# RMS norms of a 256-token network on one core: residuals and squares in two halves of 512 columns

## The chip, the cores and the metric

The kernel runs on one core of a Trainium2 chip. The core has a matrix engine (TensorE, PE in the profile; its weight loads are PEld), a vector engine (VectorE, DVE), a scalar engine (ScalarE, ACT), GpSimd (POOL) and SyncE (SP), which here only issues transfers. The engines run their own instruction streams side by side and meet at semaphores. The metric is the device time of one execution in microseconds (us); of several runs the median counts.

## The reference, cut to what matters

A batch of one sequence with S = 256 tokens and D = 1024 features passes through two blocks in float32. Every sublayer is fed by an RMS norm:

```
def rms_norm(x, g):
    y = xf * lax.rsqrt(jnp.mean(xf * xf, axis=-1, keepdims=True) + EPS)
    return y * g
first_block:   h = h + even_mixer(norm(h));  h = h + swiglu(norm(h))
               h = h + odd_mixer(norm(h));   h = h + moe_swiglu(norm(h));  h = norm_final(h)
second_block, twice:
    x = x + 0.5 * norm(swiglu_2(norm(x)));  x = x + norm(hybrid_mix(norm(x)))
    x = x + 0.5 * norm(swiglu_2(norm(x)))
```

So there are eleven norms of the residual stream itself: one of the input, three behind the plain residual additions of the first block, the final norm of the first block behind its mixture of experts, and six in the second block, each ahead of a sublayer. The first of those six stands directly behind the final norm of block one. In the second block each sublayer's output also has a norm of its own (post) before it is added; that one is not touched here.

## The kernel before, in words

The residual stream H is 128 partitions x 2 token tiles x 1024 columns; a token tile t is 128 tokens. All weights stream from memory through a ring of six buffers (SP issues, ACT rounds to a high part at L1360, DVE makes the low part at L1914), and PE multiplies high and low parts (L584, L581 for projections, L600 and L612 for the gated feed-forward, L757 and L783 for the experts).

The order of work on each engine is written out by hand; nothing is planned at run time, and every engine executes its stream in order. At each border between sublayers it is as follows.

- **DVE makes the residual.** `residual` (L2148) adds the two PSUM banks of a tile into H[:, t, :], in one instruction of 1024 columns, for t = 0 and then t = 1. In the second block `post` does it: ahead of the border it forms y * gain in HN (L2167), then for each tile a root's inverse (`inverse_root`, L1951 to L1953, and one product at L2175) and one fused multiply-add over 1024 columns (L2177). After the experts, four multiply-adds of 512 columns (L2075, `add_expert`) add the last expert. Each finished tile counts up `h_ready`.
- **ACT makes the sum of squares.** `norm` waits for `h_ready` and calls `mean_square`: a Square over 1024 columns whose accumulator gives the sum (L1379, ACTIVATE and ACTIVATION_READ_ACCUMULATOR in the trace), then a Sqrt of that sum with EPS as its bias (L1382).
- **DVE makes the diagonal.** `norm` on DVE adds EPS to the sum (L1959), takes the reciprocal of ACT's root with one Newton step (L1951 to L1953) and writes DIAG[:, t, :], the identity times the inverse root (L1962). This is behind both residual tiles in DVE's stream.
- **PE transposes and scales** at once: `turn_norm` (L815) multiplies the columns of H[:, t, :] with DIAG[:, t, :], 16 of the trace's matmuls for tile 0 and then 16 for tile 1; it has nothing else to do from the end of the old sublayer until DIAG of tile 0 is there.
- ACT (L1390) and DVE (L1971) evict the four banks into XHI and XLO with the gains, and PE starts the next sublayer.

Two borders differ. At the start, x is loaded tile by tile (`x_loaded`) and there is no residual. Behind the experts, the final norm scales H itself (L2805 to L2809: the inverse root and a multiply of 1024 columns per tile, which counts up `h_ready` again), and the next norm follows at once. The last `post` has no norm behind it: SP waits for all of `h_ready` and writes the output (L434).

Of the kernel before, what the change touches and what calls it, by code (L numbers as in the profile page):

```python
# [8 lines left out]
ALU = mybir.AluOpType  # L9
ACT = mybir.ActivationFunctionType  # L10
# [4 lines left out]
TT = S // P  # L15
D = 1024
KT = D // P
F_DENSE = 2816 // P
NE = 8
# [4 lines left out]
EPS = 1e-6  # L24
# [29 lines left out]
def build(nc, A, out):  # L54

    ctx = ExitStack()
    with ctx:
# [63 lines left out]
        H = sb("h", [P, TT, D])  # L121
# [17 lines left out]
        GBC = sb("gbc", [P, 2, D])  # L139
# [27 lines left out]
        EPS_COL, SCRATCH_COL = STAT[:, 60:61], STAT[:, 61:62]  # L167

        names = """hi_ready lo_ready chunk_used bank_free silu_ready hidhi_made
        hid_ready h_ready y_ready ssq_ready root_of_ssq y_ssq y_gained y_mean root_of_y diag_ready tp_ready xhi_ready x_ready ident_ready first_tp first_ready consts_ready cols_tp cols_ready  # L170
        loads_done gbc_used dve_order act_order pool_order router_ready msk_ready pos_mm flag_ready
        hng_ready hnh_ready hnl_ready psel_ready first_gath xgh_ready xgl_ready m_silu m_hid m_tp m_hidhi m_hidlo
        aux_mm aux_free yeh_ready yel_ready last_comb d_silu d_hid d_tp d_hidhi d_hidlo
# [198 lines left out]
        @block.sync  # L372
        def _(sp):
            def load(c_, slot, src):
                if not isinstance(c_, int) or c_ >= RING:
                    sp.wait_ge(s["lo_ready"], c_ - RING + 1)
                sp.dma_start(RAW[:, slot, :].rearrange("p (k n) -> p k n", k=src.shape[1]) if src.shape[1] * src.shape[2] == 1024
                             else RAW[:, slot, 0:src.shape[1] * src.shape[2]].rearrange("p (k n) -> p k n", k=src.shape[1]),
                             src).then_inc(raw_full[slot], 16)

            def columns(w, at_, n):
                return w[:, bass.ds(at_, n)].rearrange("(k p) n -> p k n", p=P)

            def rows(w, at_):
                return w[bass.ds(at_, P), :].rearrange("p (k n) -> p k n", k=1)

            sp.dma_start(FIRST_ROWS, vec(A["norm_mix"][0])).then_inc(first_loaded, 16)
            for t in range(TT):
                sp.dma_start(H[:, t, :], A["x"][0, t * P:(t + 1) * P, :]).then_inc(x_loaded[t], 16)
            for ph in plan:  # L390
                c0 = ph["c0"]
                if ph["kind"] == "proj":
                    for _, n, pieces in ph["units"]:
                        for i, x, k0, kn in pieces:
                            load(c0 + i, (c0 + i) % RING, columns(ph["w"][k0 * P:(k0 + kn) * P, :], x, n))
                elif ph["kind"] == "out":
                    for i, kt in enumerate(ph.get("order", range(KT))):
                        load(c0 + i, (c0 + i) % RING, rows(ph["w"], kt * P))
                elif ph["kind"] == "moe":
                    for G in range(N_GROUPS + 1):  # L400
                        e, g = divmod(G, GROUPS)
                        if G < N_GROUPS:
                            for a, w in enumerate((ph["w1"], ph["w3"])):
                                for j in range(4):
                                    c_ = m_chunk(G, 4 * a + j)
                                    src = w[e][2 * j * P:(2 * j + 2) * P, g * GW:(g + 1) * GW]
                                    load(c_, c_ % RING, src.rearrange("(k p) n -> p k n", p=P))
                        if G > 0:
                            e, g = divmod(G - 1, GROUPS)
                            for j in range(4):  # L410
                                c_ = m_chunk(G, (8 if G < N_GROUPS else 0) + j)
                                load(c_, c_ % RING, rows(ph["w2"][e], g * GW + j * P))
                else:
                    F = ph["tiles"]
                    w1, w3 = ph["w1"].rearrange("e k n -> e k n"), ph["w3"]
                    w2 = ph["w2"].rearrange("e f n -> (e f) n")

                    def w13(e, j, c_, slot):
                        for w in (w1, w3):
                            load(c_, slot % RING, columns(w[e], j * P, P))  # L420
                            c_, slot = c_ + 1, slot + 1

                    w13(0, 0, c0, c0)
                    w13(0, 1, c0 + 2, c0 + 2)
                    load(c0 + 4, (c0 + 4) % RING, rows(w2, 0))
                    with sp.Fori(1, F // 2) as i:
                        b = c0 + 6 * i - 1
                        w13(0, 2 * i, b, c0 + 5)
                        load(b + 2, (c0 + 7) % RING, rows(w2, (2 * i - 1) * P))
                        w13(0, 2 * i + 1, b + 3, c0 + 8)  # L430
                        load(b + 5, (c0 + 10) % RING, rows(w2, (2 * i) * P))
                    load(c0 + 3 * F - 1, (c0 + 3 * F - 1) % RING, rows(w2, (F - 1) * P))
            sp.wait_ge(s["h_ready"], 2 * 11)
            sp.dma_start(out[0].rearrange("(t p) d -> p t d", p=P), H[:, :, :]).then_inc(s["out_done"], 16)  # L434
            sp.wait_ge(s["out_done"], 16)

# [912 lines left out]
        def _(act):  # L1349
# [21 lines left out]

            def norm():
                for t in range(TT):
                    act.wait_ge(s["h_ready"], nxt("h_ready"))
                    mean_square(t)

            def mean_square(t):

                af(HN[:, t, :], H[:, t, :], ACT.Square, scale=D ** -0.5, accum_out=STAT[:, t:t + 1])\  # L1379
                    .then_inc(s["ssq_ready"], 1)  # L1380
                act.wait_ge(s["ssq_ready"], nxt("ssq_ready"))
                af(STAT[:, 34 + t:35 + t], STAT[:, t:t + 1], ACT.Sqrt, bias=EPS_COL).then_inc(s["root_of_ssq"], 1)  # L1382

            def gain(name):

# [473 lines left out]
            load_root()  # L1859
            for t in range(TT):  # L1860
                act.wait_ge(x_loaded[t], 16)
                mean_square(t)
            ahead(-1)
            act.wait_ge(s["first_ready"], 1)
            gain("norm_mix0")
# [34 lines left out]
        def _(dve):  # L1900
# [47 lines left out]
            def inverse_root(root, at, half, whole):  # L1948
# [4 lines left out]
                link(V_.tensor_scalar(c_, h, -half, whole, ALU.mult, ALU.add))  # L1953
                return y, c_

            def norm(keep=False):
                for t in range(TT):
                    dve.wait_ge(s["ssq_ready"], nxt("ssq_ready"))
                    link(V_.tensor_scalar(STAT[:, 36 + t:37 + t], STAT[:, t:t + 1], EPS, None, ALU.add))  # L1959
                    dve.wait_ge(s["root_of_ssq"], nxt("root_of_ssq"))  # L1960
                    y, c_ = inverse_root(STAT[:, 34 + t:35 + t], 36 + t, 0.5, 1.5)
                    V_.tensor_scalar(DIAG[:, t, :], IDENT[:, :], y, c_, ALU.mult, ALU.mult).then_inc(s["diag_ready"], 1)  # L1962
                    if keep:
                        link(V_.tensor_tensor(STAT[:, 2 + t:3 + t], y, c_, ALU.mult))
# [85 lines left out]
            def moe_sparse():  # L2050
# [81 lines left out]
                for t in range(TT):  # L2132
                    for h in range(2):
                        dve.wait_ge(s["last_comb"], 2 * t + h + 1)
                        last = add_expert(BANK[2 * t + h], NE - 1, t, h)
                    last.then_inc(s["h_ready"], 1)

            def y_wait(ph, t):

# [5 lines left out]
            def residual(ph):  # L2145
                for t in range(TT):
                    y_wait(ph, t)
                    V_.tensor_tensor(H[:, t, :], H[:, t, :], YT[t], ALU.add).then_inc(s["h_ready"], 1)  # L2148

            ngbc = [0]  # L2150

# [3 lines left out]
                ngbc[0] += 1  # L2155
                return i % 2

            def post(ph, resid):

                gi = gains_wait()  # L2160
                for t in range(TT):
# [10 lines left out]
                for t in range(TT):  # L2172
# [1 line left out]
                    y, c_ = inverse_root(STAT[:, 18 + t:19 + t], 8 + t, 0.5 * resid, 1.5 * resid)  # L2174
                    link(V_.tensor_tensor(STAT[:, 16 + t:17 + t], y, c_, ALU.mult))  # L2175
                    dve.wait_ge(s["y_gained"], nxt("y_gained", 2))
                    V_.scalar_tensor_tensor(H[:, t, :], HN[:, t, :], STAT[:, 16 + t:17 + t], H[:, t, :], ALU.mult,  # L2177
                                            ALU.add).then_inc(s["h_ready"], 1)

            def log1p(dst, e, t1, t2, t3):  # L2180

# [599 lines left out]
            V_.tensor_copy(FIRST_COLS, BANK[0][:, 0:KT]).then_inc(s["first_ready"], 1)  # L2781
            for t in range(TT):
                dve.wait_ge(x_loaded[t], 16)
            norm()
            dve.wait_ge(s["first_ready"], 1)
            ahead(-LEAD)
# [14 lines left out]

            gi = gains_wait()
            for t in range(TT):
                dve.wait_ge(s["ssq_ready"], nxt("ssq_ready"))
                link(V_.tensor_scalar(STAT[:, 36 + t:37 + t], STAT[:, t:t + 1], EPS, None, ALU.add))  # L2805
                dve.wait_ge(s["root_of_ssq"], nxt("root_of_ssq"))
                y, c_ = inverse_root(STAT[:, 34 + t:35 + t], 36 + t, 0.5, 1.5)
                link(V_.tensor_tensor(STAT[:, 2 + t:3 + t], y, c_, ALU.mult))
                V_.scalar_tensor_tensor(H[:, t, :], H[:, t, :], STAT[:, 2 + t:3 + t], GBC[:, gi, :], ALU.mult,  # L2809
                                        ALU.mult).then_inc(s["h_ready"], 1)  # L2810
            mark("gbc_used")
            mark("mixer_done")
            for l in range(2):
# [9 lines left out]
                norm()  # L2823
                gain(f"ffn2_pre{l}")
                ffn(f2)
                post(f2, 0.5)


# [32 lines left out]
```

## Time and profile before

| | us |
|---|---|
| median of 3 runs | 2709.63 (2705.88 to 2712.53) |
| the profiled execution | 2709.04 |
| its span, first to last instruction | 2707.3 |
| TensorE busy in it | 2571.3 (95%) |
| VectorE busy | 1919.0 (71%) |
| ScalarE busy | 1465.5 (54%) |
| mean granted clock of TensorE | 0.964 of full |

The difference of 1.7 us between the execution and its span lies ahead of the first and behind the last instruction. Busy shares say who could be the limit on the average; at a border between sublayers the order of the instructions and their waits decide, so those stretches have to be read by themselves.

### The profile page before, as it was taken

How to read it: one execution, taken by the hardware profiler on the slowest of the kernel's cores; microseconds unless marked ns; L12 is line 12 of the kernel's file. 1: busy time of each engine (PE TensorE's matmuls, PEld its weight loads, DVE VectorE, ACT ScalarE, POOL GpSimd, SP SyncE). 2: the span in 40 equal slices, each digit the busy share in tenths (PEclk: the TensorE clock that was granted, in tenths of full speed). 3: DMA queues.
4: the chain of work that ended last, by engine and by line, in shares of the span. 5: the costliest groups of instructions: out<-in, count | busy, mean ns of one | idle time of the engine just before them, and what ended most of it. 6: DMA issues, size and time to landing. Idle time of an engine off the chain costs nothing.

```text
span 2707.3 us, 40704 instructions
## 1 busy us (share of the span) xinstructions
PE 2571.3 (95%) x15296; PEld 2261.5 (84%) x15296; DVE 1919.0 (71%) x2609; ACT 1465.5 (54%) x1870; POOL 63.1 (2%) x137
## 2 busy tenths in 40 slices
PE   8999999699999999999999899889899899898998
PEld 8689987588888888888888799888899899787997
DVE  5555565489899989998998755687655655787554
ACT  4553353377777777777777633522533533523433
POOL 7000000000000000000000000000000000000000
PEclk9899999799999999999999899988999999989999
DMA  6255543199999999999999865422555456313553
GB/s 194 85 157 186 179 133 120 62 347 364 348 354 366 355 353 351 369 351 354 360 363 365 257 187 186 140 71 79 171 185 184 154 186 186 109 55 102 173 184 101
DMA packets 481893, 597.23 MB, mean 221 GB/s; under 512 B 21882, under 2 KB 313154, under 8 KB 481760
## 3 DMA queue, kind: packets, MB, share of 16 engines
q1 hardware_dynamic: 478048, 589.47, 64.5%
q0 software_dynamic: 3712, 6.00, 0.8%
q8 instruction: 81, 1.33, 0.2%
q14 instruction: 52, 0.43, 0.0%
HBM read 594.35 MB, written 1.05 MB: 220 GB/s over the span
## 4 chain that ended last, share of the span: by engine, by line
PE 88%; DVE 8%; ACT 2%; issue 1%; DMA 0%; DVEq 0%; SPq 0%; ACTq 0%
PE bank L600 23%; PE bank L757 23%; PE bank L783 11%; PE bank L612 11%; PE bank L584 5%; PE bank L581 2%; PE bank L815 2%; PE bank L1312 1%; DVE arena L2596 1%; PE bank L873 1%; PE bank L768 1%; DVE wlo_ring L1914 1%; PE bank L1047 1%; PE bank L704 1%; PE bank L1128 1%
## 5 line engine op out<-in xcount | busy, mean ns | idle before, releaser
L1914 DVE TENSOR_TENSOR wlo_ring<-raw_ring,whi_ring 128x1024 fp32r<-128x1024 f32 (+1 forms) x1122 | 1319.7, 1221 | 136.7 <-ACT whi_ring L1360 128.5
L1360 ACT CAST whi_ring<-raw_ring 128x1024 fp32r<-128x1024 f32 (+1 forms) x1122 | 1140.6, 1053 | 206.1 <-DMA raw_ring<-in_od_exp_w_dram 152.4
L600 PE MATMUL bank<-xhi,whi_ring 128*128 128x256 f32 x1760 | 499.6, 284 | 0.4 <-DVE xlo L1971 0.4
L600 PE MATMUL bank<-xhi,wlo_ring 128*128 128x256 f32 x1760 | 499.1, 284 | 0.0
L600 PE MATMUL bank<-xlo,whi_ring 128*128 128x256 f32 x1760 | 499.0, 284 | 0.0
L600 PEld LDWEIGHTS bank<-xhi,whi_ring 128*128 128x128 f32 x1760 | 338.0, 192 | 4.7 <-issue 0.7
L600 PEld LDWEIGHTS bank<-xlo,whi_ring 128*128 128x128 f32 x1760 | 338.0, 192 | 3.9
L600 PEld LDWEIGHTS bank<-xhi,wlo_ring 128*128 128x128 f32 x1760 | 338.0, 192 | 0.0
L1989 DVE TENSOR_TENSOR hid<-sil,bank 128x256 f32<-128x256 f32 x110 | 46.4, 422 | 402.1 <-ACT sil L1411 402.1
L1411 ACT ACTIVATE sil<-bank 128x256 f32<-128x256 f32 x110 | 42.3, 385 | 500.0 <-PE bank L600 500.0
L757 PE MATMUL bank<-whi_ring,xg0hi 128*128 128x512 f32 x448 | 180.5, 403 | 1.1 <-issue 1.1
L757 PE MATMUL bank<-whi_ring,xg1hi 128*128 128x512 f32 x448 | 180.1, 402 | 0.0
L757 PE MATMUL bank<-whi_ring,xg1lo 128*128 128x512 f32 x448 | 177.5, 396 | 0.0
L757 PE MATMUL bank<-whi_ring,xg0lo 128*128 128x512 f32 x448 | 177.5, 396 | 0.0
L757 PE MATMUL bank<-wlo_ring,xg1hi 128*128 128x512 f32 x448 | 177.4, 396 | 0.0
L757 PE MATMUL bank<-wlo_ring,xg0hi 128*128 128x512 f32 x448 | 177.3, 396 | 0.0
L584 PE MATMUL bank<-xhi,whi_ring 128*128 128x256 f32 x496 | 153.5, 309 | 0.3 <-DVE xlo L1971 0.2
L584 PE MATMUL bank<-xlo,whi_ring 128*128 128x256 f32 x496 | 146.3, 295 | 0.0
L584 PE MATMUL bank<-xhi,wlo_ring 128*128 128x256 f32 x496 | 146.3, 295 | 0.0
L783 PE MATMUL bank<-whi_ring,hidhi 128*128 128x512 f32 x448 | 139.3, 393 | 1.4 <-DVE hidlo L2097 1.4
L783 PE MATMUL bank<-whi_ring,hidlo 128*128 128x512 f32 x448 | 138.6, 391 | 0.0
L783 PE MATMUL bank<-wlo_ring,hidhi 128*128 128x512 f32 x448 | 138.2, 390 | 0.0
(502 smaller groups left out, 3858.3 us busy)
## 6 DMA issues: line engine op xcount, KB each, us to landing
raw_ring<-in_od_exp_w_dram SPq DMA_DIRECT2D x672, 512.0 KB, 5.4
raw_ring<-in_ffn_w_gate_dram SPq DMA_DIRECT2D x88, 512.0 KB, 3.9
raw_ring<-in_ffn_w_up_dram SPq DMA_DIRECT2D x88, 512.0 KB, 5.4
raw_ring<-in_ffn_w_down_dram SPq DMA_DIRECT2D x88, 512.0 KB, 5.3
raw_ring<-in_ev_ffn_w_dram SPq DMA_DIRECT2D x66, 512.0 KB, 5.2
raw_ring<-in_w_in_dram SPq DMA_DIRECT2D x42, 512.0 KB, 4.0
raw_ring<-in_od_w_in_dram SPq DMA_DIRECT2D x24, 512.0 KB, 3.9
raw_ring<-in_ev_w_in_dram SPq DMA_DIRECT2D x20, 512.0 KB, 5.2
```

Of the source, the lines that this page charges most:

```text
L581: last = mm(banks[t] if banks else row_bank(q, n, t), x[:, kt, t * P:(t + 1) * P], w[:, kk, :], start=st and (n > 256 or t == 0), stop=sp_ ...
L584: last = mm(BANK[q % 2][:, 0:S], w[:, kk, :], x[:, kt, :], start=st, stop=sp_)
L600: last = mm(BANK[qb][:, half * S:half * S + n], w[:, kt, :], x, start=(kt == 0 and a == 0), stop=(kt == KT - 1 and a == 2))
L612: last = mm(pair[h][:, :], x[:, b, t * P:(t + 1) * P], w[:, h * 512:(h + 1) * 512], start=(start and a == 0), stop=(stop and a == 2), skip ...
L704: last = mm(bank[:, q * S:(q + 1) * S], src[:, t, kt * P:(kt + 1) * P], PSEL[:, t, 2 * p:2 * p + 2, :].rearrange("p a b -> p (a b)"), star ...
L757: last = mm(bank[:, :], x[:, kt, slots], w[:, kk, :], start=(kt == 0 and a == 0), stop=(kt == KT - 1 and a == 2))
L783: last = mm(BANK[4 + h][:, :], x[:, j * P:(j + 1) * P], w[:, h * 512:(h + 1) * 512], start=(g == 0 and j == 0 and a == 0), stop=(g == GROU ...
L815: last = mm(BANK[4 + b][:, (2 * j + t) * P:(2 * j + t + 1) * P], H[:, t, kt * P:(kt + 1) * P], DIAG[:, t, :], start=True, stop=True)
L1360: nc.scalar.copy(WHI[:, slot, 0:n], RAW[:, slot, 0:n]).then_inc(s["hi_ready"], 1)
L1411: af(SIL[:, b, 0:n], BANK[b][:, 0:n], ACT.Silu).then_inc(s["silu_ready"], 1)
L1914: V_.tensor_tensor(WLO[:, slot, 0:n], RAW[:, slot, 0:n], WHI[:, slot, 0:n].bitcast(F32), ALU.subtract)\
L1989: V_.tensor_tensor(HID[:, b, 0:n], SIL[:, qb, 0:n], BANK[qb][:, S:S + n], ALU.mult)\
```

## The change

DVE writes each residual tile as two instructions of 512 columns, and each half counts up `h_ready`. ACT squares each half by itself, with a sum of its own (STAT columns t and 20 + t). DVE adds EPS to the first half's sum (`first_half`, column 22 + t, semaphore `ssq_eps`), as soon as that sum is there; ACT's Sqrt then takes the second half's sum as its input and this column as its bias. DVE's own sum for the Newton step adds the second half to it (`second_half`), where the addition of EPS stood. The places of `first_half` in DVE's stream: behind each tile's residual in `residual`, `post` (not in the last one) and behind the experts; behind each tile's arrival at the start; and in the final norm behind both scaled tiles.

```
 # ACT
-            def mean_square(t):
-                af(HN[:, t, :], H[:, t, :], ACT.Square, scale=D ** -0.5, accum_out=STAT[:, t:t + 1])\
-                    .then_inc(s["ssq_ready"], 1)
-                act.wait_ge(s["ssq_ready"], nxt("ssq_ready"))
-                af(STAT[:, 34 + t:35 + t], STAT[:, t:t + 1], ACT.Sqrt, bias=EPS_COL).then_inc(s["root_of_ssq"], 1)
+            def mean_square(t, wait_h):
+                for h in range(2):
+                    if wait_h:
+                        act.wait_ge(s["h_ready"], nxt("h_ready"))
+                    hs = slice(h * 512, (h + 1) * 512)
+                    af(HN[:, t, hs], H[:, t, hs], ACT.Square, scale=D ** -0.5,
+                       accum_out=STAT[:, 20 * h + t:20 * h + t + 1]).then_inc(s["ssq_ready"], 1)
+                act.wait_ge(s["ssq_ready"], nxt("ssq_ready", 2))
+                act.wait_ge(s["ssq_eps"], nxt("ssq_eps"))
+                af(STAT[:, 34 + t:35 + t], STAT[:, 20 + t:21 + t], ACT.Sqrt, bias=STAT[:, 22 + t:23 + t])\
+                    .then_inc(s["root_of_ssq"], 1)
 # DVE
+            def first_half(t):
+                dve.wait_ge(s["ssq_ready"], nxt("ssq_ready", 0) + 2 * t + 1)
+                V_.tensor_scalar(STAT[:, 22 + t:23 + t], STAT[:, t:t + 1], EPS, None, ALU.add).then_inc(s["ssq_eps"], 1)
+            def second_half(t):
+                dve.wait_ge(s["ssq_ready"], nxt("ssq_ready", 2))
+                dve.wait_ge(s["ssq_eps"], nxt("ssq_ready", 0) // 2)
+                link(V_.tensor_tensor(STAT[:, 36 + t:37 + t], STAT[:, 20 + t:21 + t], STAT[:, 22 + t:23 + t], ALU.add))
             def norm(keep=False):
                 for t in range(TT):
-                    dve.wait_ge(s["ssq_ready"], nxt("ssq_ready"))
-                    link(V_.tensor_scalar(STAT[:, 36 + t:37 + t], STAT[:, t:t + 1], EPS, None, ALU.add))
+                    second_half(t)
 # residual; post alike with its multiply-add, and "if not end: first_half(t)"
-                    V_.tensor_tensor(H[:, t, :], H[:, t, :], YT[t], ALU.add).then_inc(s["h_ready"], 1)
+                    for h in range(2):
+                        hs = slice(h * 512, (h + 1) * 512)
+                        V_.tensor_tensor(H[:, t, hs], H[:, t, hs], YB[t][h][:, :], ALU.add).then_inc(s["h_ready"], 1)
+                    first_half(t)
 # behind the experts
-                        last = add_expert(BANK[2 * t + h], NE - 1, t, h)
-                    last.then_inc(s["h_ready"], 1)
+                        add_expert(BANK[2 * t + h], NE - 1, t, h).then_inc(s["h_ready"], 1)
+                    first_half(t)
 # start
             for t in range(TT):
                 dve.wait_ge(x_loaded[t], 16)
+                first_half(t)
 # final norm of block one, behind the loop that scales both tiles by halves
+            for t in range(TT):
+                first_half(t)
```

## Rows read from the trace of the kernel before

**Rows 1.** Page, part 4: the chain that ended last, shares by engine.
```profile
PE 88%; DVE 8%; ACT 2%; issue 1%; DMA 0%; DVEq 0%; SPq 0%; ACTq 0%
```

**Rows 2.** Groups of instructions by form: busy us, mean ns | idle before, releaser.
```profile
L815 PE MATMUL bank<-hid,h 128*128 128x128 f32 x320 | 56.0, 357 | 57.7 <-DVE hid L1962 57.7
```

**Rows 3.** Timeline of DVE, 1728 to 1738 us: start, duration [idle before].
```profile
1730.84 1.29 DVE L2177 SCALAR_TENSOR_TENSOR h<-arena,stat,h 128x1024 f32<-128x1024 f32 x1
...
1732.92 1.28 DVE L2177 SCALAR_TENSOR_TENSOR h<-arena,stat,h 128x1024 f32<-128x1024 f32 x1
1734.12 0.15 DVE L1959 TENSOR_SCALAR stat<-stat 128x1 f32<-128x1 f32 x1
...
1735.00 0.35 DVE L1962 TENSOR_SCALAR hid<-ident,stat 128x128 f32<-128x128 f32 x1
```

**Rows 4.** Timeline of ACT, the same stretch.
```profile
1728.11 0.59 ACT L1541 ACTIVATE xlo<-bank 128x512 fp32r<-128x512 f32 x1
1728.59 0.20 ACT L1541 ACTIVATION_READ_ACCUMULATOR xlo<-bank 128x1 f32 x1
...
1732.16 1.06 ACT L1379 ACTIVATE arena<-h 128x1024 f32<-128x1024 f32 x1 [1.90 <-DVE h L2177]
1733.12 0.19 ACT L1379 ACTIVATION_READ_ACCUMULATOR arena<-h 128x1 f32 x1
1733.34 0.29 ACT L1382 ACTIVATE stat<-stat 128x1 f32<-128x1 f32 x1
```

**Rows 5.** Timelines of DVE and ACT, 150 to 164 us.
```profile
154.10 2.58 DVE L2148 TENSOR_TENSOR h<-h,bank 128x1024 f32<-128x1024 f32 x2 [4.43 <-PE bank L873]
...
156.93 0.16 DVE L1951 RECIPROCAL stat<-stat 128x1 f32<-128x1 f32 x1 [0.19 <-ACT stat L1382]
...
156.53 0.29 ACT L1382 ACTIVATE stat<-stat 128x1 f32<-128x1 f32 x1
```

**Rows 6.** Timeline of PE: the transposes at three borders.
```profile
352.06 3.84 PE L815 MATMUL bank<-hid,h 128*128 128x128 f32 x32 [2.61 <-DVE hid L1962]
...
487.17 5.47 PE L815 MATMUL bank<-hid,h 128*128 128x128 f32 x32 [2.61 <-DVE hid L1962]
...
1735.40 2.93 PE L815 MATMUL bank<-hid,h 128*128 128x128 f32 x12 [7.36 <-DVE hid L1962]
```

**Rows 7.** Groups of DVE by form.
```profile
L2075 DVE SCALAR_TENSOR_TENSOR h<-bank,arena,h 128x512 f32<-128x512 f32 x32 | 23.7, 747 | 1.8 <-PE bank L714 1.7
L2167 DVE TENSOR_TENSOR arena<-bank,gbc 128x512 f32<-128x512 f32 x24 | 15.7, 687 | 9.3 <-PE bank L612 6.8 <-PE bank L1312 2.5
L2177 DVE SCALAR_TENSOR_TENSOR h<-arena,stat,h 128x1024 f32<-128x1024 f32 x12 | 15.4, 1286 | 0.4
L2148 DVE TENSOR_TENSOR h<-h,bank 128x1024 f32<-128x1024 f32 x6 | 7.3, 1221 | 10.6 <-PE bank L1047 4.4 <-PE bank L873 4.4 <-PE bank L612 1.3
```

**Rows 8.** Timelines of ACT and DVE, 0 to 26 us.
```profile
5.04 1.06 ACT L1379 ACTIVATE arena<-h 128x1024 f32<-128x1024 f32 x1 [2.72 <-DMA h<-in_x_dram]
...
6.61 0.16 DVE L1951 RECIPROCAL stat<-stat 128x1 f32<-128x1 f32 x1
```

**Rows 9.** Timelines of ACT and DVE, 1522 to 1544 us.
```profile
1527.37 1.28 ACT L1382 ACT_TABLE_LOAD   x1
...
1524.76 2.89 DVE L2075 SCALAR_TENSOR_TENSOR h<-bank,arena,h 128x512 f32<-128x512 f32 x4 [0.84 <-PE bank L714]
...
1529.06 0.17 DVE L1951 RECIPROCAL stat<-stat 128x1 f32<-128x1 f32 x1 [1.34 <-ACT stat L1382]
...
1533.45 0.15 DVE L1959 TENSOR_SCALAR stat<-stat 128x1 f32<-128x1 f32 x1
```

**Rows 10.** Timeline of SP's queue, 2690 to 2710 us.
```profile
2702.91 0.40 SPq L434 DMA_DIRECT2D out_dram<-h  x1
```

**Rows 11.** Stretches: us, busy PE PEld DVE ACT POOL (x), PEclk, DMA share, GB/s.
```profile
352.00:356.00 4.00, 3.84 (x32) 3.65 (x32) 1.55 (x8) 1.63 (x5) 0.00 (x0) 1.00 0.00 0
...
487.00:493.00 6.00, 5.47 (x32) 5.28 (x32) 2.06 (x10) 1.97 (x7) 0.00 (x0) 0.72 0.00 0
```

More of the change, by code:

```diff
@@ L169, in build @@
         names = """hi_ready lo_ready chunk_used bank_free silu_ready hidhi_made
-        hid_ready h_ready y_ready ssq_ready root_of_ssq y_ssq y_gained y_mean root_of_y diag_ready tp_ready xhi_ready x_ready ident_ready first_tp first_ready consts_ready cols_tp cols_ready
+        hid_ready h_ready y_ready ssq_ready ssq_eps root_of_ssq y_ssq y_gained y_mean root_of_y diag_ready tp_ready xhi_ready x_ready ident_ready first_tp first_ready consts_ready cols_tp cols_ready
         loads_done gbc_used dve_order act_order pool_order router_ready msk_ready pos_mm flag_ready
@@ L432, in _ @@
                     load(c0 + 3 * F - 1, (c0 + 3 * F - 1) % RING, rows(w2, (F - 1) * P))
-            sp.wait_ge(s["h_ready"], 2 * 11)
+            sp.wait_ge(s["h_ready"], 4 * 11)
             sp.dma_start(out[0].rearrange("(t p) d -> p t d", p=P), H[:, :, :]).then_inc(s["out_done"], 16)
@@ L1373, in norm @@
                 for t in range(TT):
-                    act.wait_ge(s["h_ready"], nxt("h_ready"))
-                    mean_square(t)
-            def mean_square(t):
-                af(HN[:, t, :], H[:, t, :], ACT.Square, scale=D ** -0.5, accum_out=STAT[:, t:t + 1])\
-                    .then_inc(s["ssq_ready"], 1)
-                act.wait_ge(s["ssq_ready"], nxt("ssq_ready"))
-                af(STAT[:, 34 + t:35 + t], STAT[:, t:t + 1], ACT.Sqrt, bias=EPS_COL).then_inc(s["root_of_ssq"], 1)
+                    mean_square(t, True)
+            def mean_square(t, wait_h):
[9 more added lines that the diff above has]
+                    .then_inc(s["root_of_ssq"], 1)
             def gain(name):
@@ L1861, in _ @@
                 act.wait_ge(x_loaded[t], 16)
-                mean_square(t)
+                mean_square(t, False)
             ahead(-1)
@@ L2156, in gains_wait, with post @@
                 return i % 2
-            def post(ph, resid):
+            def post(ph, resid, end=False):
                 gi = gains_wait()
@@ L2176, in post @@
                     dve.wait_ge(s["y_gained"], nxt("y_gained", 2))
-                    V_.scalar_tensor_tensor(H[:, t, :], HN[:, t, :], STAT[:, 16 + t:17 + t], H[:, t, :], ALU.mult,
-                                            ALU.add).then_inc(s["h_ready"], 1)
+                    for h in range(2):
+                        hs = slice(h * 512, (h + 1) * 512)
+                        V_.scalar_tensor_tensor(H[:, t, hs], HN[:, t, hs], STAT[:, 16 + t:17 + t], H[:, t, hs], ALU.mult,
+                                                ALU.add).then_inc(s["h_ready"], 1)
+                    if not end:
+                        first_half(t)
             def log1p(dst, e, t1, t2, t3):
@@ L2803, in _ @@
             for t in range(TT):
-                dve.wait_ge(s["ssq_ready"], nxt("ssq_ready"))
-                link(V_.tensor_scalar(STAT[:, 36 + t:37 + t], STAT[:, t:t + 1], EPS, None, ALU.add))
+                second_half(t)
                 dve.wait_ge(s["root_of_ssq"], nxt("root_of_ssq"))
@@ L2808, in _ @@
                 link(V_.tensor_tensor(STAT[:, 2 + t:3 + t], y, c_, ALU.mult))
-                V_.scalar_tensor_tensor(H[:, t, :], H[:, t, :], STAT[:, 2 + t:3 + t], GBC[:, gi, :], ALU.mult,
-                                        ALU.mult).then_inc(s["h_ready"], 1)
+                for h in range(2):
+                    hs = slice(h * 512, (h + 1) * 512)
+                    V_.scalar_tensor_tensor(H[:, t, hs], H[:, t, hs], STAT[:, 2 + t:3 + t], GBC[:, gi, hs], ALU.mult,
+                                            ALU.mult).then_inc(s["h_ready"], 1)
+            for t in range(TT):
+                first_half(t)
             mark("gbc_used")
@@ L2825, in _ @@
                 ffn(f2)
-                post(f2, 0.5)
+                post(f2, 0.5, end=l == 1)
 _INS = ['x', 'norm_mix', 'norm_ffn', 'norm_final', 'ev_w_in', 'ev_conv_w', 'ev_conv_b', 'ev_ga_w', 'ev_ga_b',
```

## The prediction

> **What bounds the kernel now.** I read the page's chain of waits first: PE has 88% of it, DVE 8%, ACT 2% [rows 1]. So PE sets the time nearly everywhere, and work of DVE and ACT counts only where PE stands idle for it. Then the groups with their idle time: PE waits 57.7 us in all, at the ten transposes of a norm, for DVE's diagonal [rows 2]. All that the change touches lies in these waits (and in the end of the kernel, where PE is done). Last I read DVE's and ACT's timelines there, to see which instruction ends last.
>
> At a border behind a `post` [rows 3, 4] the answer is DVE. It starts the multiply-add of tile 0 at 1730.84 and that of tile 1 at 1732.92, adds EPS for tile 0 at 1734.12 and starts the diagonal of tile 0 at 1735.00, with no gap. ACT is early: its root of tile 0 started at 1733.34 and took 0.29, so it was there at 1733.63, half a microsecond ahead of the EPS addition. The reader is to see that the square of tile 0 hides behind tile 1's residual. At a border behind a plain residual [rows 5] ACT is the last, narrowly: the root started at 156.53 and ends at 156.82, and DVE's reciprocal begins at 156.93. The diagonal of tile 1 is nowhere late: PE has half of a transpose of 3.84 us or more to do first [rows 6], and in DVE's stream the small operations up to that diagonal's end take 1.2 (1734.12 to 1735.35).
>
> **The prices.** A half as against a whole on DVE: the multiply-add has 1.286 for 1024 and 0.747 for 512 columns, the plain addition 1.221 and 0.687 [rows 7]. An instruction starts 0.08 before its predecessor's end (1732.92 + 1.28 against 1734.12 [rows 3]). Two halves thus take 0.66 + 0.75 = 1.41 (+0.12) and 0.61 + 0.69 = 1.30 (+0.08).
>
> The square of a half isn't in the trace. From SBUF the whole takes 1.15 from its start to the end of the accumulator's read [rows 4]. A half from PSUM takes 0.68 (1728.11 to 1728.79), which is the lower end; half of 1.06 and a whole read, with 0.10 of overlap and a margin, makes 0.77 at most. I take 0.72, between the two. With 0.02 to reach ACT and 0.03 to come back, the first half's sum is on DVE 0.77 after that half of H is written.
>
> `first_half` is then a wait in the middle of DVE's stream. The second half of H leaves DVE free 0.58 after the first half's end (0.66 - 0.08), or 0.53 with the plain addition. So DVE stands 0.19 (0.24) and then spends 0.07 on the small operation (0.15 long, the next one overlapping). Queued behind it are the next tile's residual and, behind the second one, the whole chain to tile 0's diagonal, for which PE waits.
>
> **Border behind a `post`, five of them.** Two tiles of 0.12 + 0.19 + 0.07 make 0.76, all on the path, since DVE had no gap. `second_half` replaces the EPS addition at the same length, and its further wait costs an estimated 0.03. Together +0.79 each, +3.95. Bounds by the two ends of the square: 0.71 to 0.89.
>
> **Border behind a plain residual, three.** From 154.10: first half of H to 154.79, its sum on DVE at 155.56, H of tile 1 from 155.63, its first half done at 156.32. ACT has squared the second half of tile 0 by 156.15 and started its root at 156.18, 0.35 sooner than before; that is the gain the change makes, and DVE isn't there to take it. ACT starts the next square at 156.38, `first_half` of tile 1 goes at 157.13, `second_half` at 157.23 and the reciprocal at 157.43, where it was 156.93 [rows 5]. +0.50 each, +1.50. Bounds 0.40 to 0.60.
>
> **The start.** x of tile 0 is there at 5.04 [rows 8]. Two halves, the root and the first half of tile 1 run in a row on ACT: sum at 6.38, root at 6.41, the next square at 6.61, its sum at 7.33. DVE holds the diagonal of tile 0 back for it, since both `first_half` stand ahead of `norm`; the reciprocal goes at 7.64 instead of 6.61. +1.03.
>
> **Behind the experts, two norms in a row.** Tile 0's squares end at 1526.91, 0.45 sooner, but ACT then loads a table for 1.28 [rows 9] and computes the root until 1528.51. The first half of tile 1 waits behind both in ACT's stream, its sum comes at 1529.14, and the reciprocal of tile 0 at 1529.45 instead of 1529.06: +0.39. Two scalings by halves add 0.24, so the last is written 0.63 later; `first_half` of both tiles stands behind them, at 1534.08 where the EPS addition was at 1533.45. Here is the dearest wait: ACT's root of tile 0 needs `ssq_eps`, so it can't run before 1534.26, and behind it in ACT's stream stands the square of tile 1's first half, for which DVE's second `first_half` waits until 1535.21. The reciprocal goes at 1535.51. Before it followed the EPS addition by 0.18, at 1533.63. +1.88 in all for this border.
>
> **The end.** The last `post` has only the halves: the output is issued 0.24 later than at 2702.91 [rows 10].
>
> **Cover and what comes back.** Tile 1's diagonal is late by much the same and stays covered: at the quickest border PE needs 1.9 us for tile 0 (half of 3.84 [rows 6]), and the second diagonal ends an estimated 1.2 to 1.5 behind the first. Nothing that follows a border could absorb a late start: from each diagonal the chain is PE's own. No transfer is added or moved but the output, and the six weight buffers are full while PE waits.
>
> **Sum.** 3.95 + 1.50 + 1.03 + 1.88 + 0.24 = 8.60. On the profiled execution's 2709.04 that makes 2717.64; the median of the runs is 0.59 above it, so 2718.2, and I forecast 2718. The unknown prices move this by about -1.1 to +1.3.
>
> **Clock.** The transposes of the borders at 158 and 352 us take 3.84 each (one row stands for both [rows 6]), the other eight more: the sum of ten is 56.0 [rows 2], 17.6 above ten quick ones. The granted clock shows why: 1.00 at 352 us, all at 2.4 GHz, and 0.72 at 487, a part at 1.2 GHz [rows 11], behind equal waits of 2.61 [rows 6]. So a border is a draw of some 1.6 us, with the change or without. The Trainium skill (TensorE: Matmul & The Clock Gate, What's actually happening) says that the throttle is the default and activity releases it; by this rule longer waits can only make the clock worse, which gives the second rival. The equal waits with unlike clocks show neither for nor against it.
>
> A page speaks against the change as well. The Trainium skill (VectorE: DVE Perf Modes, The TRN2 errata) puts ScalarE from SBUF at 224 cycles plus one for each element, which makes 1.04 for the whole and an estimated 0.61 for a half. The whole took 1.06 here [rows 4], so the trace agrees; my 0.72 holds 0.63 for the half without the read, and by the page's half the sum would be 8.4.
>
> **The rivals.**
>
> *Only the added operations.* If the first half's sum came before DVE asks for it, the waits of 0.19 and 0.24 would be nothing. Then a `post` border costs 2 x 0.19 + 0.03 = 0.41, a plain one 0.15, the start about 0.5, the experts' border about 0.9, the end 0.24: 4.1 in all, 2713.7. For it: the write of H by halves may be slower than I take from PSUM forms. Against it: the root of 0.29 and the reads of 0.19 always follow the square here, and 0.68, the shortest square in the trace, is still above 0.58.
>
> *The clock falls at the quick borders too.* The two quick transposes come behind 2.61 of idle PE; with 0.5 more they may go as that at 487 did, 5.47 [rows 6]: 1.6 each, 3.3 for the transposes alone, which makes 2721.5; matmuls behind them at half clock would come on top. For it, that one of three equal borders already fell; against it, that two did not.
>
> *Not slower.* TensorE's clock comes back earlier: the borders shift against whatever the clock follows, and the low stretches in the transposes shrink. It decides from the point where 8.6 of the 17.6 us are won, that is half of all low-clock loss; the time would be 2709. The mean of the eight slower ones is 2.2 above the quick (17.6 / 8), so one border can win a microsecond, but all eight would have to. Nothing in the order of DVE's stream can give a gain of this size: the earlier roots are worth 0.35 at three borders, 1.05 in all, even if DVE were free to use them.
>
> **How the numbers follow.** The forecast has 0.56, only the added operations 0.22, the fallen clock 0.13, not slower 0.09. A measurement of this kernel tells 0.3%, 8.1 us, from no change. The forecast of 8.6 lies just beyond: with its own range, 2715.5 to 2720.5, I put 0.34 of its 0.56 on slower and 0.22 on the same. Slower: 0.34 + 0.13 = 0.47, and 0.02 from the others. Same: 0.22 + 0.20 from the second case, and 0.03 of the last. Faster 0.06. The range of 8 in 10 goes from below the first rival to beyond the second: 2712 to 2723.
>
> **What would show it.** In the trace after, behind a `post`: DVE idle by 0.2 ahead of each `first_half`, released by ACT's accumulator, and PE's wait ahead of L815 grown from 7.36 to about 8.15; behind a plain residual from 2.61 to 3.1; at the final norm the second root waiting for DVE, and PE's wait longer by 1.9. PE's wait over all ten from 57.7 to about 66. Wrong if `first_half` of tile 1 doesn't wait (then 4 us), if the half squares take nearer to 0.6, or if the transposes' sum of 56.0 moves by more than 3.

## The result and the profile after

| | before | after |
|---|---|---|
| median, us | 2707.88 (2697.58 to 2715.00, 15 runs) | 2719.34 (2713.51 to 2721.94, 15 runs) |
| ratio | 1 | 1.0045, 95% interval 1.0034 to 1.0056 |
| the profiled execution, us | 2709.04 | 2716.41 |
| its span, us | 2707.3 | 2714.7 |

The change makes the kernel 0.45% slower, 12.2 us with an interval of 9.2 to 15.2. The forecast was 8.6 us, to 2718. Medians and ratios leave out one execution of the later experiment e7, which took 8822.54 us.

The first line below is PE's group of transposes in the trace after, with busy time, mean and the idle time ahead of it, and answers to [rows 2]: PE waits 67.5 us there, not 57.7.

```profile
L815 PE MATMUL bank<-hid,h 128*128 128x128 f32 x320 | 57.9, 364 | 67.5 <-DVE hid L1977 67.5
```

PE's timeline in the trace after, at the three plain residuals and at one border behind a `post` (start, us of work, and the idle time ahead in brackets), answers to [rows 6]:
```profile
156.67 5.22 PE L815 MATMUL bank<-hid,h 128*128 128x128 f32 x32 [3.09 <-DVE hid L1977]
...
352.56 3.84 PE L815 MATMUL bank<-hid,h 128*128 128x128 f32 x32 [3.09 <-DVE hid L1977]
...
487.95 6.76 PE L815 MATMUL bank<-hid,h 128*128 128x128 f32 x32 [3.09 <-DVE hid L1977]
...
1741.15 6.51 PE L815 MATMUL bank<-hid,h 128*128 128x128 f32 x32 [8.19 <-DVE hid L1977]
```

All three plain residuals have 3.09 where they had 2.61, all five borders behind a `post` 8.19 or 8.20 where they had 7.35 or 7.36. At the start the wait is 6.37 (5.21 before), behind the experts 10.92 (7.87). DVE's timeline behind a `post` shows why, beside [rows 3]:

```profile
1735.75 1.41 DVE L2197 SCALAR_TENSOR_TENSOR h<-arena,stat,h 128x512 f32<-128x512 f32 x2
1737.29 0.15 DVE L1964 TENSOR_SCALAR stat<-stat 128x1 f32<-128x1 f32 x1
1737.36 0.15 DVE L1956 RECIPROCAL stat<-stat 128x1 f32<-128x1 f32 x1
...
1738.24 1.41 DVE L2197 SCALAR_TENSOR_TENSOR h<-arena,stat,h 128x512 f32<-128x512 f32 x2
1739.78 0.15 DVE L1964 TENSOR_SCALAR stat<-stat 128x1 f32<-128x1 f32 x1
1739.86 0.16 DVE L1970 TENSOR_TENSOR stat<-stat 128x1 f32<-128x1 f32 x1
...
1740.75 0.34 DVE L1977 TENSOR_SCALAR hid<-ident,stat 128x128 f32<-128x128 f32 x1
```

The two halves take 1.41, and `first_half` (L1964) starts 0.13 behind their end, 0.21 later than it could without a wait. ACT's timeline has the instruction it waits for. The first half's square runs from 1736.53 and its sum is read by 1737.26, 0.73 in all:

```profile
1736.53 0.63 ACT L1382 ACTIVATE arena<-h 128x512 f32<-128x512 f32 x1 [1.36 <-DVE h L2197]
1737.07 0.19 ACT L1382 ACTIVATION_READ_ACCUMULATOR arena<-h 128x1 f32 x1
...
1737.95 0.30 ACT L1386 ACTIVATE stat<-stat 128x1 f32<-128x1 f32 x1
```

The root of tile 0 is there at 1738.25, while DVE forms the next residual until 1739.65. What the halves speed up on ACT has no reader. At a plain residual DVE's timeline in the trace after names what `first_half` waits for:

```profile
153.75 0.15 DVE L1964 TENSOR_SCALAR stat<-stat 128x1 f32<-128x1 f32 x1 [0.20 <-ACT arena L1382]
...
155.30 0.15 DVE L1964 TENSOR_SCALAR stat<-stat 128x1 f32<-128x1 f32 x1 [0.21 <-ACT arena L1382]
```

Behind the experts, DVE's timeline in the trace after, beside [rows 9]:

```profile
1526.93 1.41 DVE L2090 SCALAR_TENSOR_TENSOR h<-bank,arena,h 128x512 f32<-128x512 f32 x2 [0.82 <-PE bank L714]
...
1531.34 0.15 DVE L1964 TENSOR_SCALAR stat<-stat 128x1 f32<-128x1 f32 x1 [1.41 <-ACT arena L1382]
1531.81 0.16 DVE L1970 TENSOR_TENSOR stat<-stat 128x1 f32<-128x1 f32 x1 [0.30 <-issue]
...
1536.63 0.15 DVE L1964 TENSOR_SCALAR stat<-stat 128x1 f32<-128x1 f32 x1
1537.82 0.15 DVE L1964 TENSOR_SCALAR stat<-stat 128x1 f32<-128x1 f32 x1 [1.03 <-ACT arena L1382]
...
1538.09 0.16 DVE L1956 RECIPROCAL stat<-stat 128x1 f32<-128x1 f32 x1
```
ACT's timeline of the same stretch:
```profile
1529.11 1.28 ACT L1386 ACT_TABLE_LOAD   x1
...
1536.88 0.29 ACT L1386 ACTIVATE stat<-stat 128x1 f32<-128x1 f32 x1 [1.81 <-DVE stat L1964]
```

`first_half` of tile 1 waits 1.41 behind the table load; in the second norm the root stands 1.81 for DVE's `ssq_eps`, and DVE in its turn 1.03 for the square behind that root. From the first addition to the reciprocal it is 1538.09 - 1526.93 = 11.16, and before it was 1533.63 - 1524.76 = 8.87 (the reciprocal by its 0.18 behind the last of [rows 9]). That is 2.29 more, while PE's wait grew by 3.05: PE's last matmul ahead of it ended 1.34 behind DVE's first addition (1539.19 - 10.92 - 1526.93), and 2.10 behind it in the trace before. Such a shift of up to 1 us in PE's wait behind the experts also stands between the experiments' traces (1.33 in e7, 2.35 in e4). DVE's chain doesn't follow it: it takes 8.86 in e8, where PE ends 1.35 behind the first addition.

### The profile page after: what moved, and what is told of

It reads as the page before. It is cut to its first block, busy times and chain, and to the rows that moved or that the text cites. A ratio compares the mean times of both kernels' runs of the same rounds, so it can differ in the third digit from the quotient of the medians.

```text
span 2714.7 us, 40833 instructions
## 1 busy us (share of the span) xinstructions
PE 2568.8 (95%) x15296; PEld 2258.3 (83%) x15296; DVE 1925.0 (71%) x2651; ACT 1472.8 (54%) x1914; POOL 63.9 (2%) x137
## 3 DMA queue, kind: packets, MB, share of 16 engines
q8 instruction: 81, 1.33, 0.2%
## 4 chain that ended last, share of the span: by engine, by line
PE 88%; DVE 8%; ACT 2%; issue 1%; DMA 0%; DVEq 0%; SPq 0%; ACTq 0%
PE bank L600 23%; PE bank L757 23%; PE bank L783 11%; PE bank L612 11%; PE bank L584 5%; PE bank L581 2%; PE bank L815 2%; PE bank L1312 1%; PE bank L873 1%; PE bank L768 1%; DVE arena L2618 1%; PE bank L1047 1%; DVE wlo_ring L1919 1%; PE bank L704 1%; PE bank L1128 1%
```

## The experiments

The ratios are against runs of the kernel before on the same chip, whose median was between 2706.2 and 2707.1. "Wait" is PE's idle time ahead of its ten transposes, from one trace each; 57.7 before, 67.5 after.

| kernel | median, us | ratio, interval | wait, us |
|---|---|---|---|
| e1_tile1_late | 2713.06 | 1.0021, 1.0008 to 1.0034 | 61.5 |
| e2_halves_only | 2707.05 | 1.0004, 0.9992 to 1.0016 | 59.7 |
| e3_whole_residual | 2729.52 | 1.0077, 1.0056 to 1.0098 | 74.8 |
| e4_diag_between | 2699.94 | 0.9978, 0.9966 to 0.9990 | 54.7 |
| e5_between_whole | 2704.40 | 0.9992, 0.9979 to 1.0004 | 55.5 |
| e7_table_early | 2705.32 | 0.9988, 0.9975 to 1.0001 | 55.3 |
| e8_busy_wait | 2695.31 | 0.9954, 0.9937 to 0.9972 | 36.2 |
| e9_all | 2696.77 | 0.9963, 0.9950 to 0.9975 | 34.9 |
| e11_after_busy | 2712.42 | 1.0023, 1.0014 to 1.0033 | 44.4 |
| e10_busy_all | 2694.67 | 0.9952, 0.9938 to 0.9965 | 20.2 |
| e12_after_quick | 2715.45 | 1.0029, 1.0019 to 1.0039 | 63.1 |

**Tile 1's wait behind tile 0's diagonal.**
```
 # behind each residual, at the start, in the final norm
-                    first_half(t)
+                    if t == 0:
+                        first_half(t)
 # second_half
+                if t:
+                    V_.tensor_scalar(STAT[:, 22 + t:23 + t], STAT[:, t:t + 1], EPS, None, ALU.add).then_inc(s["ssq_eps"], 1)
```


> As the changed kernel, but the EPS addition of tile 1 stands behind tile 0's diagonal, so DVE waits in the middle of its stream only for tile 0. Theory (the wait for tile 1's first sum delays tile 0's diagonal, DVE being in order): PE's wait at the transposes falls from 67.5 to about 61.5 over the ten: behind a post from 8.19 to 7.93, behind a plain residual from 3.09 to 2.75, at the start from 6.37 to 5.35, at the final norm from 10.92 to about 8.2. Rival (only the added operations count): 0.07 for each border less, so 66.8. Rival (TensorE's clock made the difference): the waits may fall, and the time doesn't follow.

```profile
L815 PE MATMUL bank<-hid,h 128*128 128x128 f32 x320 | 55.5, 354 | 61.5 <-DVE hid L1979 61.5
```
The wait is 61.5, as the theory had it, and 66.8 would have been the rival's. Behind a `post` it is 7.89 and behind a plain residual 2.71, each within 0.05 of the theory; 4.98 at the start and 8.95 behind the experts, where 5.35 and 8.2 were expected, nearly cancel. The time follows, from 12.2 above the kernel before to 5.7 (2.2 to 9.2). One wait, moved by a few small instructions in DVE's stream, is 6 of the 10 us of wait.

**The halves alone.**
```
-                act.wait_ge(s["ssq_eps"], nxt("ssq_eps"))
-                af(..., STAT[:, 20 + t:21 + t], ACT.Sqrt, bias=STAT[:, 22 + t:23 + t])
+                af(..., STAT[:, 20 + t:21 + t], ACT.Sqrt, bias=STAT[:, t:t + 1])
 # DVE: no first_half; in place of second_half
+                dve.wait_ge(s["ssq_ready"], nxt("ssq_ready", 2))
+                link(V_.tensor_scalar(STAT[:, 36 + t:37 + t], STAT[:, 20 + t:21 + t], STAT[:, t:t + 1], EPS,
+                                      ALU.add, ALU.add))
```


> Halves of the residual and of the squares as in the changed kernel, but no first_half: ACT's root takes the first sum itself as its bias (EPS is left out of the root's estimate; DVE still adds it to the sum of the Newton step in one operation with both sums). No wait in the middle of DVE's stream. Theory (the waits are the larger part, the halves themselves 0.12 a tile): PE's wait about 59.2 over the ten, 7.66 behind a post, 2.61 behind a plain residual, 5.35 at the start, 7.7 at the final norm; time 1.5 to 2 above the kernel before. Rival (the halves are the cost, by more events and smaller instructions): the waits stay near 67.5 and the time near the changed kernel's.

```profile
L815 PE MATMUL bank<-hid,h 128*128 128x128 f32 x320 | 56.9, 360 | 59.7 <-DVE hid L1971 59.7
```
59.7, within half a microsecond of the theory; the time can't be told from the kernel before. So of the 9.8 us that PE waits longer in the changed kernel, 7.8 come with `first_half`: its waits, its small operations and the wait for `ssq_eps`. The other 2.0 stand in this trace too, but not all of them are the halves: 0.7 is behind the experts, where DVE's chain didn't grow (8.82 against 8.87) and PE's last matmul ended 1.35 behind the first addition instead of 2.10.

**The suspected wait made larger.**
```
                 for h in range(2):
-                    if wait_h:
+                    if wait_h and h == 0:
                         act.wait_ge(s["h_ready"], nxt("h_ready"))
 # DVE: residuals in one instruction of 1024 columns as in the kernel before, first_half kept
```


> As the changed kernel with first_half and the halved squares, but DVE writes each residual tile whole, as before: the first half's square can start only when the whole tile is written, so the suspected wait grows from 0.19 to about 0.85 a tile while the split of the residual is gone. Theory: PE's wait behind a post grows to about 9.23, behind a plain residual to 4.1, over the ten to about 76, and the time is some 8 above the changed kernel. Rival (only added operations): fewer of them, so 59 to 60 over the ten and nearly the time of before.

DVE's timeline behind a `post`:
```profile
1744.61 1.29 DVE L2194 SCALAR_TENSOR_TENSOR h<-arena,stat,h 128x1024 f32<-128x1024 f32 x1
1746.69 0.15 DVE L1964 TENSOR_SCALAR stat<-stat 128x1 f32<-128x1 f32 x1 [0.79 <-ACT arena L1382]
```
The wait is visible as a gap of 0.79, twice a border, and PE waits 74.8 with fewer instructions than in the changed kernel. The rival by which only added operations count has fallen. Both transposes that took 3.84 in the trace before, at the first two plain residuals, take 5.46 and 5.47 here, behind waits of 4.13. The time is 20.8 above the kernel before (15.2 to 26.5), with 17.1 of it in the waits.

**The order on DVE.**
```
 # e4: in post (not the last) and in the final norm, between the halves
                     for h in range(2):
                         V_.scalar_tensor_tensor(H[:, t, hs], ...).then_inc(s["h_ready"], 1)
+                        if t and h == 0 and not end:
+                            norm_tile(0)
 # e5: the kernel before, whole, with norm_tile(0) ahead of tile 1's residual
+                    if t and not end:
+                        norm_tile(0)
                     V_.scalar_tensor_tensor(H[:, t, :], HN[:, t, :], ...)
```


> e2_halves_only, and behind each post and in the final norm DVE makes the diagonal of tile 0 between the two halves of tile 1's residual. If DVE's order is what sets the border: PE's wait behind a post 7.02 (0.34 less than before), at the final norm about 7.05, elsewhere as in e2_halves_only, 55.3 over the ten; time 2 below the kernel before. The diagonal of tile 1 comes about 3.2 behind tile 0's, just covered by a transpose at the lower clock (3.0 to 3.3 for half of it) and late by up to 1.3 where the clock is high. Rival (the root on ACT sets the border): no change against e2_halves_only.

> The kernel before with whole residuals and whole squares; only the diagonal of tile 0 is moved in DVE's stream ahead of tile 1's residual, behind each post and in the final norm. Theory (DVE's order sets tile 0's diagonal, and halves are needed only to keep tile 1's close behind): the first wait behind a post falls from 7.36 to about 6.8, but tile 1's diagonal comes 3.8 behind it, so PE waits a second time, 0.75 where the transposes run at the lower clock and up to 1.9 at the higher; the time 0 to 4 above the kernel before, so 6 or more above e4_diag_between. Rival (the order alone gives e4's gain, the halves give nothing): as fast as e4_diag_between.

e4's wait behind a `post` was 7.00 to 7.02, at the final norm 6.91, 54.7 in all, and it is the first that beats the kernel before, by 6 us (2.7 to 9.2). Expected were 2, and the waits give 3.0, so that a part of the 6 isn't explained. Of e5 the trace confirms the two parts and refutes the price. PE's timeline at 2315 us:
```profile
2315.85 3.61 PE L815 MATMUL bank<-hid,h 128*128 128x128 f32 x16 [6.78 <-DVE hid L1961]
2319.69 2.05 PE L815 MATMUL bank<-hid,h 128*128 128x128 f32 x16 [0.24 <-DVE hid L1961]
```
6.78 is the forecast 6.8, and tile 1's diagonal comes 3.8 later. But half a transpose at the lower clock takes 3.61, where I had 3.0, so almost nothing is left to wait for; it was the only second wait of its ten. The measured time lies 2 below the kernel before (5.7 below to 1.1 above), where 0 to 4 above was expected. That the halves add anything to the new order isn't shown: the intervals of e4 and e5 overlap, and the waits differ by 0.8 (54.7 against 55.5). The rival by which the order alone gives the gain stands.

**The table.**
```
                 moe_sparse()
+            load_root()
             norm()
```


> e4_diag_between, ACT loads the root's table ahead of the final norm while it is idle, and the last post writes its residual whole again. Theory: the first norm behind the experts is then held by DVE's four multiply-adds, so PE's wait there falls from 6.91 to about 6.2, and the output is issued 0.24 sooner; 0.9 in all against e4_diag_between, which its measurement can hardly tell; the trace has to show it. Rival (the table load was not on the path): the wait stays 6.9.

DVE's timeline behind the experts in this trace:
```profile
1520.24 2.73 DVE L2088 SCALAR_TENSOR_TENSOR h<-bank,arena,h 128x512 f32<-128x512 f32 x4 [0.83 <-PE bank L714]
...
1528.09 0.34 DVE L1971 TENSOR_SCALAR hid<-ident,stat 128x128 f32<-128x128 f32 x1
```
and in e4's:
```profile
1520.91 3.13 DVE L2087 SCALAR_TENSOR_TENSOR h<-bank,arena,h 128x512 f32<-128x512 f32 x4 [0.82 <-PE bank L714]
...
1529.77 0.34 DVE L1970 TENSOR_SCALAR hid<-ident,stat 128x128 f32<-128x128 f32 x1
```
From the first addition to the diagonal it is 7.85 here and 8.86 in e4's. So the table was on the path, worth 1.0. PE's wait stayed at 6.92 all the same, because its last matmuls ahead of it ended sooner in this run. The whole kernel wasn't faster than e4 (2705.32 against 2699.94, a ratio of 0.9988 against 0.9978); an effect of 1 us can't be seen in it, and the other difference isn't explained. As e7 has e4's order of DVE and its gain isn't clear of zero, e4's 6 us have to be taken with care.

**A busy PE.**
```
-            def turn_norm():
+            def turn_norm(idle=0):
+                for i in range(idle):
+                    mm(BANK[0][:, 0:P], IDENT[:, :], IDENT[:, :], start=True, stop=True)
                 for t in range(TT):
 # e8, e9, e11: idle=20 behind each post; e12: idle=6 at the three plain residuals
 # e10: 12 at the start, 6 at the plain residuals, 24 behind the experts (bank 7), 20 behind each post
```


> The kernel before; in the wait behind each of the five posts PE first computes 20 products of the identity with itself into a bank that is free, some 4.8 us at the higher clock, so that it idles 2.5 and not 7.4. Nothing of the norm changes. If idleness of PE costs clock at these borders: the transposes there run at 3.84 instead of 5.3 to 6.8, PE's L815 sum falls from 56.0 to about 44.5, and the time falls by some 11. If the clock doesn't follow PE's idle time: same sum, same time.

> e7_table_early with the products of e8_busy_wait: the version that should beat both kernels. If both effects add: 11 from the clock, 6 to 7 from the order, so 16 to 18 below the kernel before. The diagonal of tile 1 comes 3.2 behind tile 0's and half a quick transpose takes 1.9, so up to 1.3 at each of five borders may be given back: then 10 to 12 below.

PE's timeline in e8 at a border behind a `post`, the products on the identity first:
```profile
1723.50 4.62 PE L811 MATMUL bank<-ident 128*128 128x128 f32 x40
...
1731.01 3.84 PE L817 MATMUL bank<-hid,h 128*128 128x128 f32 x32 [2.88 <-DVE hid L1964]
```
PE's timeline in e9 at such a border:
```profile
2489.09 2.05 PE L817 MATMUL bank<-hid,h 128*128 128x128 f32 x16 [2.54 <-DVE hid L1973]
2491.98 2.05 PE L817 MATMUL bank<-hid,h 128*128 128x128 f32 x16 [0.84 <-DVE hid L1973]
```
e8 is 12.4 below its kernel before (7.6 to 17.1), where some 11 were expected, though only two of its five such transposes took 3.84 (the others 5.28 to 6.76) and their sum fell to 50.4, not 44.5; the rest of the gain lies outside the transposes and wasn't located. In e9 half a transpose at the higher clock is over in 2.05 and PE stands 0.84 for tile 1's diagonal. The two gains don't add: e9 is 10 below (6.8 to 13.5), not 16 to 18. That is the smaller of the two expected outcomes, and no better than e8 alone.

> The changed kernel with the 20 products of e8_busy_wait in PE's wait behind each of the five posts; it differs from e8_busy_wait by the change alone, at borders where the clock no longer falls. If the change costs what the waits show (0.84 behind a post, 0.48 behind a plain residual, 1.1 at the start, 2.3 at the final norm, 0.26 at the end: 9.3), it is 9 to 10 above e8_busy_wait's 2695.3, so 2704.5. If a good part of the 12 between the changed kernel and the one before was clock lost in longer waits, it is 9 or less above; if the longer remaining wait (3.7 instead of 2.9) lets the clock fall again, it comes to 2710 or more.

> e8_busy_wait, and such products at the other borders too (12 ahead of the first transposes, while x is loaded; 6 at the three plain residuals; 24 behind the experts), and ACT loads the root's table early behind the experts. Norms as in the kernel before. If a busy PE keeps or gets the clock: the first transposes take 3.84 instead of 6.29 and the projections behind them are quicker, the experts' border saves about 1 by the table and 2 by the clock; 4 to 9 below e8_busy_wait. If clock in those stretches follows something else, the same as e8_busy_wait.

e11 is 17 above e8 by the medians, 19 by the ratios. The steps of the waits are 9.3 of it (8.2 in PE's waits, 44.4 against 36.2). The other 8 to 9 are clock as far as the traces show: the transposes take 55.5 instead of 50.4, and the mean granted clock over the runs is 0.970 against 0.975; 3 to 4 us outside the transposes weren't located. This is the third of the expected outcomes, 2710 or more. PE then idles 3.73 where it idled 2.88:
```profile
1742.11 5.46 PE L817 MATMUL bank<-hid,h 128*128 128x128 f32 x32 [3.72 <-DVE hid L1979]
```
All five transposes behind a `post` took 5.46 or 5.47. e10 has every gap but those behind `post` shorter, transposes of 3.84 or less at eight of ten borders and 42.8 for all ten, yet its time is that of e8: 2694.67 against 2695.31, and 4 to 9 less were expected. Why the quicker transposes don't show in the time wasn't found.

> The changed kernel with 6 products of the identity (1.4 us) in PE's wait at the three plain residuals only, so that PE idles about 1.7 there instead of 3.09. If the longer waits of the change cost clock at these borders: the first two transposes take 3.84 each, as in the kernel before (5.22 and 3.84 in the changed kernel's trace), and the time is 2 to 4 below the changed kernel's 1.0045 of before, so 1.0030 to 1.0037. If the clock there isn't lost to the waits: 1.0045 again, and transposes as likely above 3.84 as without.

```profile
156.18 3.84 PE L817 MATMUL bank<-hid,h 128*128 128x128 f32 x32 [1.75 <-DVE hid L1979]
350.67 3.84 PE L817 MATMUL bank<-hid,h 128*128 128x128 f32 x32 [1.74 <-DVE hid L1979]
486.36 3.84 PE L817 MATMUL bank<-hid,h 128*128 128x128 f32 x32 [1.75 <-DVE hid L1979]
```
All three at 3.84, and 1.0029 instead of 1.0045, 4.3 us; the two intervals overlap (e12's reaches up to 1.0039, the change's down to 1.0034), so the size is uncertain and the direction likely. Not all of the 4.3 is a loss of the change: the third transpose took 5.47 already in the kernel before, so 1.6 of what e12 wins there the kernel before doesn't have either.

The stretch from the transposes at the first plain residual to those behind the experts shows it without the rest of the kernel. It takes 1376.7 in the trace before and 1376.2 in e8, which is the same program there; 1382.5 in the changed kernel and 1382.1 in e11, which are the same program there; 1379.6 in e12. So the changed kernel is 5.8 slower in it. The steps give 0.48 + 0.48 + 2.29 = 3.3 of that, and the transposes that took 5.22 for 3.84 and 6.76 for 5.47 about the rest, 2.7. In e12 2.9 are left, about the steps alone. So, as far as one trace of each can show it, lengthening these waits by 0.48 costs clock as well.

## Why the prediction was right, point by point

- **The mechanism.** `first_half` in the middle of DVE's in-order stream delays tile 0's diagonal. Shown by e1 (wait moved: 61.5), e2 (wait gone: 59.7) and e3 (wait enlarged: 74.8), all against expectations within 1.2 us in the sum, and within 0.05 at every border behind a `post` or a plain residual.
- **The prices.** Two half multiply-adds 1.41, forecast 1.41. Half a square with its read 0.73, forecast 0.72. A `post` border +0.84 (forecast 0.79), a plain one +0.48 (0.50), the end +0.26 (0.24: from the first residual's start to the last's end 3.64 against 3.38).
- **The start.** From the first square to the transposes 3.87 against 2.76, +1.11, forecast 1.03; in the trace after, the square started 0.08 later because x did.
- **Behind the experts.** In DVE's chain +2.29, forecast 1.88. The step that was mis-sized is the first norm: 5.07 from the first addition to the reciprocal against 4.30, +0.77 where the prediction had 0.39. `first_half` went 4.41 behind the first addition, exactly as worked out, but `second_half` followed it by 0.47 and not by 0.08. Of that 0.30 is issue, and its cause is open. DVE's stream leaves the branch over the experts' two variants there, but in e3 `first_half` waits as long at the same place, and `second_half` follows it by 0.10:
```profile
1541.02 0.15 DVE L1964 TENSOR_SCALAR stat<-stat 128x1 f32<-128x1 f32 x1 [1.36 <-ACT arena L1382]
...
1541.12 0.16 DVE L1970 TENSOR_TENSOR stat<-stat 128x1 f32<-128x1 f32 x1
```
- **The sum.** 5 x 0.84 + 3 x 0.48 + 1.11 + 2.29 + 0.26 = 9.3, forecast 8.6. PE's ten waits grew by 9.8 (forecast 66, measured 67.5): without the end, but with the 0.76 by which PE's last matmuls behind the experts ended sooner.
- **The clock.** The measured loss is 12.2, so about 2.9 more than the steps, with 3 either way. The prediction held this as its second rival, apart from the forecast, at 0.13, and put nothing of it into the sum. It called a border a draw of 1.6 us, with the change or without, and that was wrong: in all eight traces with a wait of 2.6 to 2.7 at the plain residuals the first two transposes took 3.84 and the third 5.46 or 5.47. With 3.1 to 4.1 (after, e11, e3) five of the six at the first two borders took 5.22 to 5.47. So forecast and rival held together, and adding a part of the rival to the forecast would have been better than choosing between them. The sum of the ten transposes moved from 56.0 to 57.9, within the 3 that the prediction allowed.
- **Luck.** That 2719.34 lies 1.1 from the forecast of 2718.2 is in part luck. By the medians the loss is 11.5, and the sum of 8.6 lacks 2.9 of it. But the forecast started from the median of three runs, 2709.63, and that of fifteen was 2707.88; the too high start hid 1.75 of these 2.9.
- **The chances.** 0.45% is beyond 0.3%, on which 0.49 was set; 0.45 stood on no change, mostly because 8.6 lay on the border of what can be told.

Open is what lies outside the stretch of 5.8 us above. From the first transposes to the end of PE's work ahead of the second border no change touches anything, and single traces took between 143.1 (e4) and 148.3 (e2) for it; 147.6 in the trace before and 144.6 in that after. By this the two profiled executions lie only 7.4 apart, less than the steps, and one pair of traces can't give the size of the loss.

## What to carry to other kernels

A semaphore wait in an in-order stream is paid by everything queued behind it, so a partial sum that is early for its producer can be late for its reader: place the consumer where its input is already there, and ask what stands behind it. Splitting work between two engines can pay only if the receiving engine's order lets it start sooner: the halves alone (e2) changed nothing that can be measured, and with the diagonal of tile 0 moved up (e4) the kernel was quicker than before. The move without the halves (e5) can't be told from that. Count PE's idle gaps by length, not only by sum, and price the clock with them.

## What the runs showed of the hardware

Transposes (32 matmuls of the trace) by PE's idle time ahead of them, at the plain residuals and in e11 behind `post`: behind 1.27 to 1.75 us all six took 3.84 (e10, e12); behind 2.6 to 2.7 the first two borders 3.84 and the third 5.46 or 5.47, alike in the kernel before, e1, e2, e4, e5, e7, e8 and e9; behind 3.09 in the changed kernel 5.22, 3.84 and 6.76, in e11 5.46, 5.47 and 5.34; behind 3.73 (e11, five times) 5.46 or 5.47; behind 4.13 (e3) 5.46, 5.47 and 6.33. Behind 2.88 or 2.89 (e8 and e10, behind `post`) five of ten took 3.84 and the others 5.28 to 6.76. 3.84 is the level of 2.4 GHz in this case [rows 11]. So a longer wait goes with slower transposes, but its length alone doesn't settle them. The Trainium skill (TensorE: Matmul & The Clock Gate, What's actually happening) says that activity releases the throttle. These rows agree as far as that goes, and so does e8, whose mean granted clock was 0.975 over its runs against 0.965 for the kernel before (26 runs).

Behind a wait of 1.41 at the end of the experts DVE's next instruction but one came 0.46 to 0.47 later in the changed kernel, e11 and e12, with 0.30 of it issue, and 0.10 later in e3 behind a wait of 1.36. What makes the difference isn't known.
